# Filler multiplies of the identity on TensorE, at five changes of stage and in the two softmaxes of a sample attention

## The chip, the cores and the metric

The kernel runs on one core of a Trainium2 chip. The metric is the device time of one execution in microseconds. Three runs of the kernel before gave 2719.67, 2724.30 and 2724.41 us; the median is 2724.3 us. TensorE (PE in the profile) multiplies; its weight loads are a row of their own (PEld). VectorE (DVE), ScalarE (ACT) and GpSimd (POOL) do the element work, SyncE (SP) issues most DMAs. The profile also says which clock TensorE was granted: 1.00 stands for 2.4 GHz and 0.50 for 1.2 GHz.

## What is computed

One layer of a decoder for a prompt of 2048 tokens and 8 samples of 4 new tokens each, width 1024. Cut to what matters:

```python
h = rms_norm(x, norm1_g) * (1 + sc1) + sh1
q, k, v, u = split(h @ w_in)                 # w_in: 1024 x 2560
q, k = rms_norm(q per head), rms_norm(k per head)
o_attn = attend(q, k, v)                     # three dilated window patterns, merged by their softmax sums
glu = u[..., :512] * sigmoid(u[..., 512:])
o_conv = silu(layer_norm(causal_depthwise_conv31(glu))) @ w_pw2
x = x + g1 * (concat(o_attn, o_conv) @ w_o)
h2 = rms_norm(x, norm2_g) * (1 + sc2) + sh2
x = x + g2 * (square(relu(h2 @ w_ff1)) @ w_ff2)   # 1024 -> 4096 -> 1024
```

The prompt's attention works on its own keys, the samples' attention on a cache of 2048 positions each. The outputs are x, the new keys and values, and the last rows of glu.

## The kernel before

The work is cut into stages. Each is a block in which every engine has its own list of instructions in the order in which the code writes it; there is no scheduler. Semaphores join the lists. A tile is 128 tokens (`NT` = 16 tiles of the prompt, and a seventeenth of the 32 sample tokens). The stages are, with the prefix that their tiles carry in the profile:

1. `vu_`: modulation, first norm, the products for v and u, glu and most of the convolution;
2. `qk_`: the products for q and k, their norms, and their transposition. It starts with the sample tile: for each of 8 slices of the weights ACT writes the high part (`qk_w_hi`), DVE the low part (`qk_w_lo`, L1314), and TensorE multiplies as they come;
3. `pa_`: the prompt's attention. Beside it POOL gathers keys into `pa_key_run` (L1573) and does the rest of the convolution (L1577, L1578);
4. `sa_`: the samples' attention in two groups of four samples. For each group TensorE transposes cached keys (L1886), multiplies scores (L1898, L1905), then waits for a softmax on DVE and ACT, transposes the probabilities (`values`, L1911 to L1917) and multiplies them by the values (L1929, L1935);
5. `mx_`: mixing of the three patterns, convolution output, output projection, residual and second norm. The last step of TensorE is `turn_x(NT)` (L2435, transposes of L2441) for the sample tile;
6. `ff_`: the feed-forward products, from 1289 us to nearly the end.

Between two stages stands `end_stage()` (L125). The block's own end is a barrier: each engine first drains, that is, it finishes what it has been given, then reports, and goes on when all five have reported. Then the stage's semaphores are cleared, and a second barrier of the same kind follows (L129). An engine that is late at the first holds all the others. SP comes to the barrier only when the stores that the next stage reads have landed, or when they are issued, depending on the stage.

TensorE multiplies float32 numbers in two ways here. Where both operands carry the type fp32r, as in the large products, a call of `matmul` is one row of the trace; where they are plain float32, as in L1017, it is two rows. A `transpose` of float32 is one row.

In `qk_`, `turn_qk(NT)` (L1358) is the last step of TensorE: it waits for the tile's queries, transposes four blocks, waits for the keys (`nrm_done`), and transposes four more.

Of the kernel before, what the change touches and what calls it, by code (L numbers as in the profile page):

```python
# [15 lines left out]
P = 128  # L16
# [78 lines left out]
def build(nc, I, O):  # L95
# [22 lines left out]
    with whole:  # L118
# [15 lines left out]
        ident = keep("ident", [P, P])  # L134
# [32 lines left out]
        def copy_part(eng, i):  # L167

            n, part = divmod(i, COPY_PARTS)
            name, out = (("cache_k", "new_k_sample"), ("cache_v", "new_v_sample"))[n % 2]  # L170
            src = I[name][0, n // 2].rearrange("r h d -> (r h d)")[DS * AW:WINC * AW]
            dst = O[out][0, n // 2].rearrange("r h d -> (r h d)")[0:(WINC - DS) * AW]
            rows = slice(part * 16, (part + 1) * 16)
            a = 16 * COPY_PARTS
            eng.dma_start(dst.rearrange("(a n) -> a n", a=a)[rows], src.rearrange("(a n) -> a n", a=a)[rows]).then_inc(parts_copied, 16)

        class Chain:

# [41 lines left out]
        with conv:  # L220
# [454 lines left out]
            with ExitStack() as st:  # L675
# [35 lines left out]
                with nc.Block() as block:  # L711
# [252 lines left out]
                    def _(pe):  # L964
# [77 lines left out]
                        for i in range(2, NT + 1):  # L1042
# [6 lines left out]
                                partial(i)  # L1049
                            turn_glu(i - 1)  # L1050
                        turn_glu(NT)

            front.close()
            end_stage()
# [42 lines left out]
            with ExitStack() as st:  # L1097
# [47 lines left out]
                with nc.Block() as block:  # L1145
# [193 lines left out]
                    def _(pe):  # L1339
# [18 lines left out]
                        def turn_qk(u):  # L1358
                            n = rows_of(tile_at[u])
                            if u < NT:  # L1360
                                pe.wait_ge(nrm_done, u + 1)
                            if u >= 1:
                                pe.wait_ge(t_done, u)
                            for half in range(2):
                                if u == NT:
                                    if half == 0:
                                        pe.wait_ge(z_free, NT + 1)
                                    else:
                                        pe.wait_ge(nrm_done, NT + 1)
                                for c in range(4):  # L1370
                                    mm = pe.transpose(t_ps[:, half, c, 0:n], nrm[0:n, u % 2, (4 * half + c) * P:(4 * half + c + 1) * P], ident[0:n, 0:n])
                                mm.then_inc(t_pe, 1)

                        for u in range(NT):
                            products(u)
                            if u >= 2:
                                turn_qk(u - 2)
# [2 lines left out]
                        products(NT, (1,))  # L1380
                        turn_qk(NT - 1)
                        turn_qk(NT)

            end_stage()
            both.close()

            with ExitStack() as st:
# [111 lines left out]
                with nc.Block() as block:  # L1499
# [102 lines left out]
                    def _(pe):  # L1602
# [48 lines left out]
                        for s in range(STEPS + 4):  # L1651
                            if s < STEPS:
                                scores(2 * s)
                                scores(2 * s + 1)
                            if 1 <= s < STEPS + 1:
                                turn(2 * s - 2)
                                turn(2 * s - 1)
                            if s >= 4:
                                back(s - 4)
                            if 2 <= s < STEPS + 2:  # L1660
                                weigh(2 * s - 4)
                                weigh(2 * s - 3)

                    @block.vector
                    def _(v):
# [95 lines left out]
        with ExitStack() as st:  # L1761
# [26 lines left out]
            o_ps = ps("o_ps", [P, 512])  # L1788
# [20 lines left out]
            with nc.Block() as block:  # L1809
# [68 lines left out]
                def _(pe):  # L1878
# [27 lines left out]
                        mm.then_inc(s_pe, 1)  # L1906

                    def values(g):
                        pe.wait_ge(s_exp, 3 * g + 3)
                        for m in range(4):  # L1910
                            mm = pe.transpose(p_ps[1][:, m * P:(m + 1) * P], prob[:, 2, DS + m * P:DS + (m + 1) * P], ident[:])  # L1911
# [3 lines left out]
                            mm = pe.transpose(p_ps[0][:, m * P:(m + 1) * P], prob[:, 0, m * P:(m + 1) * P], ident[:])  # L1915
                        mm.then_inc(p_pe, 1)
                        pe.transpose(k_ps[0][0:DS, 0, :], prob[:, 0, 4 * P:SKEYS], ident[:]).then_inc(p_pe, 1)  # L1917
                        if g >= 1:
                            pe.wait_ge(o_done, g)
                        for a in range(2):  # L1920
                            if a == 0:
                                pe.wait_ge(p_cp, 2 * g + 2)
# [12 lines left out]
                                    pe.matmul(o_ps[part, :], probN[:, part], vnew[:, G * g + j, :], start=False, stop=False)  # L1935
                        mm.then_inc(o_pe, 1)

                    for g in range(DB // G):
                        for n in range(2 * G * g, 2 * G * (g + 1)):
                            for c in range(4):  # L1940
                                turn(n, c)
                            if n == 2 * G * g + G:
                                scores(2 * g)
                        scores(2 * g + 1)
                        values(g)

                @block.vector
                def _(v):
# [86 lines left out]
        with ExitStack() as st:  # L2035
# [57 lines left out]
            with nc.Block() as block:  # L2093
# [294 lines left out]
                def _(pe):  # L2388
# [77 lines left out]
                    for i in range(NT + 1):  # L2466
                        if i < NT:
                            turn_dw(i + 1)
                        project(i, 0)
                        if i < NT:  # L2470
                            turn_y(i + 1)
                            turn_o(i + 1)
                        project(i, 1)
                        if i >= 1:
                            turn_x(i - 1)
                    turn_x(NT)

        end_stage()
        lent.close()

        with ExitStack() as st:
# [199 lines left out]
            with nc.Block() as block:  # L2681
# [447 lines left out]
                def _(pe):  # L3129
# [19 lines left out]
                    def three(out, s, m, hi, lo, first, last, more=False):  # L3149
# [2 lines left out]
                        pe.matmul(out, w_hi[:, s % WR, w], lo, start=False, stop=False, skip_group_check=more)  # L3152
                        return pe.matmul(out, w_lo[:, s % WR, w], hi, start=False, stop=last, skip_group_check=more)  # L3153

                    for b in range(NB_ALL):
                        run, blk = divmod(b, BLKS)
                        w = RUNS[run][1]
# [112 lines left out]
```

## Time and profile before

| | |
|---|---|
| median of 3 runs | 2724.3 us |
| time of the profiled execution | 2723.36 us |
| its span, first to last instruction | 2721.5 us |
| PE busy | 2579.1 us (95%) |
| PEld busy | 2283.1 us (84%) |
| DVE, ACT, POOL busy | 1717.0, 1220.9, 1122.9 us |
| mean granted TensorE clock | 0.974 |

The span lies 1.9 us below the execution's own time. PE's busy share counts a matmul from its start to the end of its last result, so that neighbours overlap; it says that TensorE nearly always had something to do, not that it ran at its peak. The clock of 0.974 is a mean: it was 1.00 in most of the span and 0.50 in a handful of stretches of 3 to 27 us, the longest of them before 60 us, in the first stage.

### The profile page before, as it was taken

How to read it: one execution, taken by the hardware profiler on the slowest of the kernel's cores; microseconds unless marked ns; L12 is line 12 of the kernel's file. 1: busy time of each engine (PE TensorE's matmuls, PEld its weight loads, DVE VectorE, ACT ScalarE, POOL GpSimd, SP SyncE). 2: the span in 40 equal slices, each digit the busy share in tenths (PEclk: the TensorE clock that was granted, in tenths of full speed). 3: DMA queues.
4: the chain of work that ended last, by engine and by line, in shares of the span. 5: the costliest groups of instructions: out<-in, count | busy, mean ns of one | idle time of the engine just before them, and what ended most of it. 6: DMA issues, size and time to landing. Idle time of an engine off the chain costs nothing.

```text
span 2721.5 us, 45843 instructions
## 1 busy us (share of the span) xinstructions
PE 2579.1 (95%) x16346; PEld 2283.1 (84%) x16346; DVE 1717.0 (63%) x3931; ACT 1220.9 (45%) x3063; POOL 1122.9 (41%) x771
## 2 busy tenths in 40 slices
PE   6999989998999689997899999999999999999998
PEld 3678857876777546875899999999999999999998
DVE  3268889987888437875555555555555555555555
ACT  3444323458888324554434433433443343344332
POOL 0000000008997006653555545535554553555543
PEclk7999999998999889998999999999999999999999
DMA  8756625843445873673423443352454335235222
GB/s 287 276 201 230 206 104 199 269 128 113 137 137 160 301 313 121 196 240 93 146 75 136 171 137 117 100 195 71 139 171 136 117 105 186 82 131 190 78 63 82
DMA packets 314671, 431.24 MB, mean 158 GB/s; under 512 B 23546, under 2 KB 243430, under 8 KB 307910
## 3 DMA queue, kind: packets, MB, share of 16 engines
q1 hardware_dynamic: 292570, 378.88, 41.9%
q0 software_dynamic: 4272, 39.19, 4.1%
q10 hardware_dynamic: 17604, 10.24, 1.2%
q8 instruction: 133, 2.18, 0.3%
q14 instruction: 92, 0.75, 0.1%
HBM read 353.72 MB, written 146.65 MB: 184 GB/s over the span
## 4 chain that ended last, share of the span: by engine, by line
PE 43%; issue 2%; DVE 2%; DMA 2%; POOL 1%; ACT 1%; SPq 1%; DVEq 0%; POOLq 0%; ACTq 0%
PE ff_u_ps L3151 15%; PE ff_u_ps L3152 14%; PE ff_u_ps L3153 14%; DMA gluT<-h_d 1%; POOL ff_w_lo L2796 1%; DMA out_y_prompt_dram<-ff_x_own 0%; DVE ff_wT L3008 0%; SPq L2714 0%; ACT ff_h_hi L2853 0%; ACT ff_w_hi L2844 0%; POOL ff_h_lo L2805 0%; DMA ff_x_own<-x_d 0%; PE ff_out_ps L3146 0%; DVE ff_x_own L3033 0%; DVE ff_wT L2970 0%
## 5 line engine op out<-in xcount | busy, mean ns | idle before, releaser
L2796 POOL TENSOR_TENSOR ff_w_lo<-gluT,ff_w_hi 128x512 fp32r<-128x512 f32 x342 | 458.1, 1347 | 409.2 <-ACT ff_w_hi L2844 409.2
L3151 PE MATMUL ff_u_ps<-ff_a_hi,ff_w_hi 128*128 128x352 f32 (+1 forms) x1536 | 493.4, 321 | 10.7 <-POOL ff_a_lo L2811 8.8
L3152 PE MATMUL ff_u_ps<-ff_a_lo,ff_w_hi 128*128 128x352 f32 (+1 forms) x1536 | 493.5, 321 | 0.0
L3153 PE MATMUL ff_u_ps<-ff_a_hi,ff_w_lo 128*128 128x352 f32 (+1 forms) x1536 | 493.1, 321 | 0.0
L3151 PE MATMUL ff_u_ps<-ff_h_hi,ff_w_hi 128*128 128x352 f32 (+1 forms) x1368 | 441.4, 323 | 16.0 <-DVE ff_h_lo L2956 8.1
L3153 PE MATMUL ff_u_ps<-ff_h_hi,ff_w_lo 128*128 128x352 f32 (+1 forms) x1368 | 437.8, 320 | 0.0
L3152 PE MATMUL ff_u_ps<-ff_h_lo,ff_w_hi 128*128 128x352 f32 (+1 forms) x1368 | 437.1, 320 | 0.0
L3051 DVE SCALAR_TENSOR_TENSOR ff_y<-ff_u_ps,modT,ff_y 128x352 f32<-128x352 f32 (+2 forms) x336 | 188.2, 570 | 314.2 <-PE ff_u_ps L3153 314.2
L2796 POOL TENSOR_TENSOR ff_w_lo<-ff_wT,ff_w_hi 128x512 fp32r<-128x512 f32 x168 | 225.4, 1344 | 272.2 <-ACT ff_w_hi L2844 172.5
L2844 ACT ACTIVATE ff_w_hi<-gluT 128x512 fp32r<-128x512 f32 x342 | 211.4, 626 | 274.8 <-PE ff_u_ps L3153 257.4
L3151 PEld LDWEIGHTS ff_u_ps<-ff_a_hi,ff_w_hi 128*128 128x128 f32 x1536 | 290.5, 189 | 12.7 <-POOL ff_a_lo L2811 10.0
L3153 PEld LDWEIGHTS ff_u_ps<-ff_a_hi,ff_w_lo 128*128 128x128 f32 x1536 | 290.2, 189 | 0.0
L3152 PEld LDWEIGHTS ff_u_ps<-ff_a_lo,ff_w_hi 128*128 128x128 f32 x1536 | 290.1, 189 | 0.0
L3151 PEld LDWEIGHTS ff_u_ps<-ff_h_hi,ff_w_hi 128*128 128x128 f32 x1368 | 258.0, 189 | 23.4 <-issue 12.0
L3152 PEld LDWEIGHTS ff_u_ps<-ff_h_lo,ff_w_hi 128*128 128x128 f32 x1368 | 257.9, 189 | 0.0
L3153 PEld LDWEIGHTS ff_u_ps<-ff_h_hi,ff_w_lo 128*128 128x128 f32 x1368 | 256.9, 188 | 0.0
L2844 ACT ACTIVATE ff_w_hi<-ff_wT 128x512 fp32r<-128x512 f32 x168 | 105.6, 632 | 320.0 <-PE ff_u_ps L3153 234.6
L1735 ACT ACTIVATE pa_score<-pa_score,pa_stat 128x256 f32<-128x256 f32 (+1 forms) x384 | 172.3, 451 | 36.3 <-DVE pa_stat L1680 34.6
L287 DVE SCALAR_TENSOR_TENSOR vu_dwp<-gluT,tapT,vu_dwp 128x512 f32<-128x512 f32 x240 | 161.0, 745 | 0.8 <-DVE rstd L204 0.8
L985 PE MATMUL vu_z_ps<-vu_w_hi,last_hi 128*128 128x512 f32 (+1 forms) x384 | 152.0, 396 | 2.5 <-DVEq L923 2.5
L986 PE MATMUL vu_z_ps<-vu_w_lo,last_hi 128*128 128x512 f32 (+1 forms) x384 | 150.3, 391 | 0.0
L987 PE MATMUL vu_z_ps<-vu_w_hi,last_lo 128*128 128x512 f32 (+1 forms) x384 | 150.0, 391 | 0.0
(354 smaller groups left out, 5016.3 us busy)
## 6 DMA issues: line engine op xcount, KB each, us to landing
gluT<-in_w_ff_dram SPq DMA_DIRECT2D x192, 512.0 KB, 5.0
out_new_k_sample_dram<-in_cache_k_dram SPq DMA_DIRECT2D x40, 511.0 KB, 6.1
out_new_v_sample_dram<-in_cache_v_dram SPq DMA_DIRECT2D x40, 511.0 KB, 6.3
dwq<-in_w_ada_dram SPq DMA_DIRECT2D x32, 512.0 KB, 8.8
gluT<-in_cache_k_dram SPq DMA_DIRECT2D x16, 1024.0 KB, 8.6
gluT<-h_d SPq DMA_DIRECT2D x80, 176.0 KB, 5.2
mx_acc<-acc_d SPq DMA_DIRECT2D x16, 768.0 KB, 8.1
out_new_k_sample_dram<-in_cache_k_dram POOLq DMA_DIRECT2D x3, 4088.0 KB, 16.6
```

Of the source, the lines that this page charges most:

```text
L287: return v.scalar_tensor_tensor(out=out, in0=x, scalar=tap(j, c), in1=out, op0=ALU.mult, op1=ALU.add)
L985: pe.matmul(z, hi, w_hi[:, k, cols], start=k == 0, stop=False)
L986: pe.matmul(z, hi, w_lo[:, k, cols], start=False, stop=False)
L987: mm = pe.matmul(z, lo, w_hi[:, k, cols], start=False, stop=k == KT - 1)
L1735: act.activation(prob[:, u % 4, hh, cols], score[:, u % 4, hh, cols], ACT.Exp, bias=stat[:, p, t, 0, h:h + 1], scale=-1.0, accum_out=stat[ ...
L2796: pool.tensor_tensor(slot_view(w_lo, s), src, slot_view(w_hi, s).bitcast(F32), ALU.subtract).then_inc(w_lod, 1)
L2844: act.activation(slot_view(w_hi, s), src, ACT.Copy).then_inc(w_hid, 1)
L3051: ins = v.scalar_tensor_tensor(out=dst, in0=src[:, 0:gated], scalar=g2, in1=dst, op0=ALU.mult, op1=ALU.add)
L3151: pe.matmul(out, w_hi[:, s % WR, w], hi, start=first, stop=False, skip_group_check=more)
L3152: pe.matmul(out, w_hi[:, s % WR, w], lo, start=False, stop=False, skip_group_check=more)
L3153: return pe.matmul(out, w_lo[:, s % WR, w], hi, start=False, stop=last, skip_group_check=more)
```

## The change

A helper issues `n` plain float32 multiplies of the 128 x 128 identity by itself, into a part of PSUM that nobody reads any more or yet. It is called at twelve places: behind the last step of TensorE in the first five stages (24, 30, 30, 34 and 24 calls of `matmul`), at the start of three stages (8, 8 and 12), ahead of the last half of `turn_qk(NT)` (18), ahead of `turn_x(NT)` in `mx_` (50), and twice in each of the two softmaxes (26 and 8). In `values` the wait for `o_done` moves to the front, since the fillers write the bank that this semaphore guards. Nothing is removed.

```diff
+        def keep_awake(pe, out, n):
+
+            for _ in range(n):
+                pe.matmul(out, ident[:], ident[:], start=True, stop=True)
@@ end of vu_ @@
                         turn_glu(NT)
+                        keep_awake(pe, xt_ps[:, 0], 24)
@@ qk_, turn_qk @@
                                     if half == 0:
                                         pe.wait_ge(z_free, NT + 1)
                                     else:
+                                        keep_awake(pe, z_ps[0][:, 0:P], 18)
                                         pe.wait_ge(nrm_done, NT + 1)
@@ qk_, start and end @@
+                        keep_awake(pe, z_ps[5][:, 0:P], 8)
                         for u in range(NT):
                             products(u)
...
                         turn_qk(NT)
+                        keep_awake(pe, z_ps[0][:, 0:P], 30)
@@ end of pa_ @@
+                        keep_awake(pe, s_bank[0][0][:, 0:P], 30)
@@ sa_, values @@
                     def values(g):
+                        if g >= 1:
+                            pe.wait_ge(o_done, g)
+                        keep_awake(pe, o_ps[:, 0:P], 26)
                         pe.wait_ge(s_exp, 3 * g + 3)
...
                         pe.transpose(k_ps[0][0:DS, 0, :], prob[:, 0, 4 * P:SKEYS], ident[:]).then_inc(p_pe, 1)
-                        if g >= 1:
-                            pe.wait_ge(o_done, g)
+                        keep_awake(pe, o_ps[:, 0:P], 8)
@@ sa_, start and end @@
+                    keep_awake(pe, o_ps[:, 0:P], 8)
                     for g in range(DB // G):
...
                         values(g)
+                    keep_awake(pe, k_ps[1][:, 0], 34)
@@ end of mx_ @@
+                    keep_awake(pe, dw_ps[:, 0:P], 50)
                     turn_x(NT)
+                    keep_awake(pe, dw_ps[:, 0:P], 24)
@@ start of ff_ @@
+                    keep_awake(pe, out_ps[:, 0:P], 12)
```

The order in which the instructions stand on TensorE at three of the places follows. A row is a line of the code, an operation, output and inputs, and how many times in a row; the numbers at the left count rows. After the change all later lines have higher numbers (L1371 is L1378, L1911 is L1924, L2441 is L2455); the fillers are L180.

TensorE at the end of `qk_` and the start of `pa_`, before: `qk_t_ps` holds the transposed queries and keys.

```order
2144 L1355 MATMUL qk_z_ps<-qk_w_hi,last_lo 128x512
2145 L1371 MATMUL qk_t_ps<-ident,qk_nrm 128x128 x16
2146 L1145 UNCONDITIONAL_BRANCH
2147 L1601 UNCONDITIONAL_BRANCH
2148 L1615 MATMUL pa_s_ps<-first_k,first_q 128x128 x2
```

The same place after the change:

```order
2146 L1361 MATMUL qk_z_ps<-qk_w_hi,last_lo 128x512
2147 L1378 MATMUL qk_t_ps<-ident,qk_nrm 128x128 x12
2148 L180 MATMUL qk_z_ps<-ident 128x128 x18
2149 L1378 MATMUL qk_t_ps<-ident,qk_nrm 128x128 x4
2150 L180 MATMUL qk_z_ps<-ident 128x128 x30
2151 L1151 UNCONDITIONAL_BRANCH
2152 L1610 UNCONDITIONAL_BRANCH
2153 L1624 MATMUL pa_s_ps<-first_k,first_q 128x128 x2
```

Of the last sixteen transposes the last four now stand behind 18 fillers, and the way to the barrier behind 30.

TensorE in the first softmax of `sa_`, before: `sa_s_ps` are the scores, `sa_k_ps` the transposed probabilities, `sa_o_ps` the output.

```order
2556 L1898 MATMUL sa_s_ps<-sa_kTt,sa_qblk 32x512 x16
2557 L1911 MATMUL sa_k_ps<-ident,sa_prob 128x128 x4
2558 L1915 MATMUL sa_k_ps<-ident,sa_prob 128x128 x4
2559 L1917 MATMUL sa_k_ps<-ident,sa_prob 4x128
2560 L1929 MATMUL sa_o_ps<-first_v,sa_probT 32x512 x3
```

The same place after the change:

```order
2563 L1908 MATMUL sa_s_ps<-sa_kTt,sa_qblk 32x512 x16
2564 L180 MATMUL sa_o_ps<-ident 128x128 x26
2565 L1924 MATMUL sa_k_ps<-ident,sa_prob 128x128 x4
2566 L1928 MATMUL sa_k_ps<-ident,sa_prob 128x128 x4
2567 L1930 MATMUL sa_k_ps<-ident,sa_prob 4x128
2568 L180 MATMUL sa_o_ps<-ident 128x128 x8
2569 L1941 MATMUL sa_o_ps<-first_v,sa_probT 32x512 x3
```

The transposes of the probabilities stand behind 26 fillers, the products with the values behind 8 more.

TensorE at the end of `mx_` and the start of `ff_`, before: `mx_h_ps` holds the transposed second norm.

```order
3495 L2441 MATMUL mx_h_ps<-ident,mx_x1n 128x128 x8
3496 L2441 MATMUL mx_h_ps<-ident,mx_x1n 128x32 x8
3497 L2093 UNCONDITIONAL_BRANCH
3498 L3128 UNCONDITIONAL_BRANCH
3499 L3151 MATMUL ff_u_ps<-ff_h_hi,ff_w_hi 128x352
```

The same place after the change:

```order
3507 L2455 MATMUL mx_h_ps<-ident,mx_x1n 128x128 x8
3508 L180 MATMUL mx_dw_ps<-ident 128x128 x50
3509 L2455 MATMUL mx_h_ps<-ident,mx_x1n 128x32 x8
3510 L180 MATMUL mx_dw_ps<-ident 128x128 x24
3511 L2107 UNCONDITIONAL_BRANCH
3512 L3144 UNCONDITIONAL_BRANCH
3513 L180 MATMUL ff_out_ps<-ident 128x128 x12
3514 L3167 MATMUL ff_u_ps<-ff_h_hi,ff_w_hi 128x352
```

The sample tile's eight transposes stand behind 50 fillers, the barrier behind 24, and the first product of `ff_` behind 12.

## Rows read from the trace of the kernel before

**Rows 1.** Windows: length, busy PE, PEld, DVE, ACT, POOL, granted clock, DMA share, GB/s.
```profile
394.00:412.00 18.00, 9.78 (x24) 3.17 (x25) 11.08 (x18) 8.13 (x8) 0.00 (x0) 0.62 0.59 206
...
sum 85.00, PE 43.44 PEld 27.66 DVE 33.39 ACT 28.78 POOL 13.79; mean PE 6.21 PEld 3.95 DVE 4.77 ACT 4.11 POOL 1.97
```

**Rows 2.** Group of line L1017 (busy us, mean ns), and weight loads by start.
```profile
L1017 PE MATMUL vu_q_ps<-vu_sel,vu_part 128*128 128x9 f32 x48 | 6.3, 241 | 0.0
...
162.96 0.53 PEld L1017 LDWEIGHTS vu_q_ps<-vu_sel,vu_part 128*128 128x128 f32 x4
163.40 0.19 PEld L985 LDWEIGHTS vu_z_ps<-vu_w_hi,last_hi 128*128 128x128 f32 x1
```

**Rows 3.** From `vu_` to `qk_`: instructions by start, duration; a wait of SP.
```profile
392.84 1.01 SPq L771 DMA_DIRECT2D out_new_conv_sample_dram<-vu_glu  x1
393.56 0.40 PE L996 MATMUL vu_g_ps<-ident,vu_glu 32*128 32x32 f32 x4 [1.64 <-DVE gluT L940]
397.36 1.06 ACT L1259 ACTIVATE qk_w_hi<-dwq 128x1024 fp32r<-128x1024 f32 x1 [5.25 <-PEq L129]
...
SPq L776 <- DMA out_new_conv_sample_dram<-vu_glu: 2.2, 1, 2.2
```

**Rows 4.** From `qk_` to `pa_`, in order of time.
```profile
611.25 0.66 PE L1371 MATMUL qk_t_ps<-ident,qk_nrm 128*128 128x128 f32 x4 [3.03 <-ACT qk_qkT L1233]
615.26 1.12 PE L1371 MATMUL qk_t_ps<-ident,qk_nrm 128*128 128x128 f32 x4 [3.35 <-DVE qk_nrm L1310]
620.99 2.01 POOL L1573 COPY pa_key_run<-first_k 128x1024 f32<-128x1024 f32 x1 [119.70 <-POOLq L129]
```

**Rows 5.** In `pa_`, a wait of PE and POOL's first gap.
```profile
750.09 1.23 PE L1615 MATMUL pa_s_ps<-pa_key_run,pa_query_run 64*128 64x128 f32 x8 [2.81 <-POOL pa_key_run L1573]
...
865.93 1.98 POOL L1573 COPY pa_key_run<-pa_kT 128x1024 f32<-128x1024 f32 x1 [1.60 <-PE pa_s_ps L1615]
```

**Rows 6.** From `pa_` to `sa_`, PE.
```profile
901.90 0.41 PE L1648 MATMUL pa_o_ps<-ident,pa_oT 128*128 128x128 f32 x2 [0.61 <-DVE pa_o_sb L1697]
908.05 1.30 PE L1886 MATMUL sa_k_ps<-ident,gluT 128*128 128x128 f32 x5 [5.74 <-PEq L129]
```

**Rows 7.** The first softmax of `sa_`, in order of time.
```profile
941.08 3.64 PE L1898 MATMUL sa_s_ps<-sa_kTt,sa_qblk 128*32 128x512 f32 x32
948.17 1.11 PE L1911 MATMUL sa_k_ps<-ident,sa_prob 128*128 128x128 f32 x4 [3.45 <-ACT sa_prob L2016]
950.86 0.27 DVE L1985 COPY sa_probN<-sa_k_ps 4x128 f32<-4x128 f32 x1
951.18 1.08 PE L1929 MATMUL sa_o_ps<-first_v,sa_probT 128*32 128x512 f32 x3 [0.83 <-DVE sa_probN L1985]
952.04 1.07 PE L1929 MATMUL sa_o_ps<-first_v,sa_probT 128*32 128x512 f32 x3
954.93 0.60 PE L1929 MATMUL sa_o_ps<-first_v,sa_probT 128*32 128x512 f32 x3
955.36 0.60 PE L1929 MATMUL sa_o_ps<-first_v,sa_probT 128*32 128x512 f32 x3
```

**Rows 8.** From `sa_` to `mx_`, in order of time.
```profile
1001.45 0.61 PE L1929 MATMUL sa_o_ps<-sa_vn,sa_probT 128*32 128x512 f32 x3
1003.95 2.70 SPq L1852 DMA_DIRECT2D os_d<-sa_o_r  x4
1009.94 0.60 ACT L2247 ACTIVATE gluT<-mx_f_ps 128x512 f32<-128x512 f32 x1 [18.80 <-PE mx_f_ps L2450]
```

**Rows 9.** From `mx_` to `ff_`, in order of time.
```profile
1271.63 1.03 PE L2441 MATMUL mx_h_ps<-ident,mx_x1n 128*128 128x128 f32 x8
1281.09 1.05 PE L2441 MATMUL mx_h_ps<-ident,mx_x1n 32*128 32x32 f32 x8 [8.43 <-DVE mx_x1n L2325]
1284.92 0.58 SPq L2148 DMA_DIRECT2D h_d<-gluT  x1
1286.84 0.63 ACT L2844 ACTIVATE ff_w_hi<-gluT 128x512 fp32r<-128x512 f32 x1 [9.42 <-PEq L129]
```

## The prediction, made before the changed kernel ran

> **What bounds the kernel now.** I read the page first, then the granted clock in windows over the whole span, then, at each place that the change touches, the timeline of every engine across the gap. The first view shows that TensorE has nearly always something to do; the second, what there is to win. From 394 us on, seven stretches with a lowered clock lie at the places of the change. Together they last 85 us, and PE is busy in 43.4 of them [rows 1]; the first has a mean clock of 0.62, the others are like it. Work at the lower level takes twice as long, so a clock that never fell could give back half of the busy time, some 20 us, and that only where PE's work sets the pace. The timelines then show what does set the pace in each gap: a store that SP waits for, a norm on DVE, a softmax on ACT, or the barrier. In front of these PE is idle for 3 to 8 us. A filler is free as long as it ends before what PE waits for; each 0.1 us beyond is paid in full, since a barrier holds five engines. So the question is how long a filler lasts.
>
> **The price of a filler.** Of L1017, a plain float32 multiply with 128 x 128 weights, the trace has 48 rows [rows 2]; the code calls it 24 times (two calls for each of twelve groups). A call is two rows, two weight loads and two matmuls. Four such loads, two calls, take from 162.96 to 163.40 us, so 0.11 us a row at full clock. With 128 columns to move, as the filler has, eight float32 rows of L2441 take 1.03 us, (1.03 - 0.27) / 7 = 0.11 us each with 0.27 us for the last one's end [rows 9]. Loads and matmuls overlap, so a row costs 0.11 and a call 0.22 us. No row shows both sizes in one plain multiply. The lower bound is one row a call, 0.11 us; the upper is a load that hides behind nothing, 0.11 + 0.11 a row, 0.44 a call. I take 0.22, which both nearest rows give.
>
> The Trainium skill ("TensorE: Matmul & The Clock Gate", Part 2, on the back-to-back issue gap) gives about 56 ns for a single matmul of 128 columns at full clock and 81 ns for a pair of load and matmul in a stream. By the first, estimated, 24 calls would last 1.3 us and no filler would end late; the time would be that of the first rival below. The trace does not agree for this kind: two calls of L1017 took 0.44 us [rows 2], and the measurement decides.
>
> **The barrier.** Before 397.36 SP had issued its last store at 392.84 + 1.01 and waited 2.2 us for it: it arrived at 396.05 and ACT began 1.31 us later [rows 3]. At 1284.92 + 0.58 = 1285.50 SP had issued the last store of `mx_`, and ACT began 1.34 us later [rows 9]. So the next stage begins 1.33 us after the last engine arrives. PE arrives when its last matmul has ended, 0.16 us after its last slot (0.27 less 0.11).
>
> **Place by place**, fillers at 0.22 us:
>
> 1. `vu_` to `qk_`: PE is free at 393.8. 24 calls, 5.3 us, end at 399.3 against the arrival of SP at 396.05: **+3.2**. What then starts later is ACT's and DVE's splitting of weights, from which PE's first products wait; a warm PE only waits longer there. The 8 calls at the start, 1.8 us, stand beside ACT's 1.06 us and DVE's first split: at most 0.5 more, taken as 0.
> 2. `turn_qk(NT)` and the end of `qk_`: the first four transposes end at 611.25 + 0.44. 18 calls, 4.0 us, end at 615.7 where the keys had been waited for until 615.26: 0.4 late, and the four cold transposes (1.12 us, the last 0.42 of it an end) become 0.3 us faster or more. That cancels. From 616.1 the 30 calls last 6.6 us, to 622.9; the others arrive at 620.99 - 1.33 = 619.7 [rows 4]: **+3.2**.
> 3. In `pa_` the first 6 us run faster at full clock, 2 to 3 us of PE's work. But POOL works without a gap from 620.99 to its first wait, ahead of 865.93, and at 750.09 PE waits 2.8 us for POOL's `pa_key_run` [rows 5]. What PE gains before is waiting time there: **0**. This hides the gain, and if POOL were not the pace, up to 3 us would come back.
> 4. `pa_` to `sa_`: PE is free at 902.1; 30 calls end at 908.9 against 908.05 - 1.33 = 906.7 [rows 6]: **+2.2**. The 8 calls ahead of the first transposes stand beside loads that DVE waits for: 0.
> 5. The first softmax: the scores end at 944.5 (eight slots of 0.43 us from 941.08). 26 calls last to 950.2, where the probabilities were ready at 948.17 [rows 7]: 2.0 late. Nine warm transposes end at 951.2, 8 calls at 953.0, and DVE's copy is ready before; the products with the values begin 1.8 us later than at 951.18. Their first four slots are then warm: 952.04 - 951.18 = 0.86 becomes 955.36 - 954.93 = 0.43, 1.7 us won. Net **+0.1**. The second softmax, 982 to 1002 us, repeats the pattern with 3.5 cold slots: **+0.3**.
> 6. `sa_` to `mx_`: PE is free at 1001.9; 34 calls, 7.5 us, and the end of the last: 1009.5 against SP's arrival at 1003.95 + 2.70 = 1006.65 [rows 8]: **+2.9**. In `mx_` the first transposes are warm, and ACT, which paces the next 3 us, starts its first copy some 0.85 us earlier than 1009.94: **-0.85**.
> 7. Ahead of `turn_x(NT)`: PE is free at 1271.63 + 0.88 = 1272.5. 50 calls, 11.0 us, end at 1283.5; the norm was ready at 1281.09 [rows 9]: 2.4 late, less 0.5 as these transposes are now warm. The path on is DVE, SP's store, barrier. But behind the transposes, at 1284.0, stand 24 calls, 5.3 us, to 1289.5 with their end. The arrival was 1285.50: **+4.0**. The 12 calls at the start of `ff_` last 2.7 us, as long as PE has to wait for ACT and DVE there: 0.
>
> The sum: 3.2 + 3.2 + 2.2 + 0.1 + 0.3 + 2.9 - 0.85 + 4.0 = 15.05 us. On the profiled execution's own 2723.36 us that is 2738.4, and since the median of the runs is 0.9 us above it I forecast **2739 us**. `ff_` runs as before. Where its pace falls on the clock's own steps, a few us of PE at 1333 or 2289 us may turn warm or cold by chance: +-2 us.
>
> **Rivals.**
>
> A. The fillers fit. A call costs one row's 0.11 us, because the plain multiply of so small a size is one slot. Then the 24 calls end at 396.7 (+0.6), the 18, 26, 30, 34, 50 and 24 all before what is waited for. Each softmax wins 2.6 us (0.9 in the transposes, 1.7 in the products), `mx_` 0.85, the end of `qk_` 0.4 and `turn_x(NT)` 0.5: 0.6 - 5.2 - 1.75 = -6.35, **2718 us**. For it: all the gaps in question are 1.2 to 2 times as long as the fillers at that price. Against it: the 48 rows for 24 calls [rows 2]. The point from which it decides is a price of 0.17 us a call: there the places 1, 2, 4, 6 and 7 run over by 2.0, 1.3, 0.7, 1.2 and 0.4 us and the softmaxes by 0.75 each, 7.1 in all, against 7.0 won. Below it the kernel is not slower.
>
> B. The clock falls all the same, before or within a filler, and the filler runs at the lower level, 0.44 us a call. The likeliest place is ahead of the 18 calls, where PE has been idle for 3.0 us [rows 4]. If the 30 calls there and the 24 of place 1 run cold, 6.6 + 5.3 us more: **2750 us**.
>
> C. The late stage catches up. `sa_` waits for its loads and `ff_` for its own, and what had been issued ahead of the barrier goes on while PE fills. If both take their whole delay back, 2.2 + 4.0 less: **2733 us**. Against it: SP stands at the barrier as well and issues nothing.
>
> **Chances.** Forecast 0.66 (its own range 2732 to 2745), A 0.14, B 0.08, C 0.12. The range that leaves out no more than 2 in 10 is 2724 to 2752: it cuts off A, and holds B and C with the clock's steps. What a measurement of this kernel can tell from no change is 0.2%, 5.4 us, so from 2718.9 to 2729.7. A lies at its lower edge and goes two thirds to faster, one third to the same; the low end of C and half-fitting fillers add to the same: faster 0.10, same 0.09, slower 0.81.
>
> **What would show it.** In the profile after, L180 has 612 rows for 306 calls, starts 0.11 us apart. The clock is 1.00 at 613 to 627, 947 to 955, 988 to 996 and 1275 to 1293 (all shifted). The next stage begins 1.3 us after the last L180 at the five changes of stage. `pa_` from POOL's first row to PE's last is as long as before, with a longer wait at the place of 750. I am wrong if L180 has 306 rows, if its rows start less than 0.07 us apart, or if stages begin while the fillers run. A lowered clock within the fillers would be B.

## The result and the profile after

The changed kernel takes **2741.1 us** (median of 4 runs, 2740.75 to 2741.21) against 2724.4 us before (4 runs, 2719.67 to 2726.86): a ratio of **1.0070**, 95% interval 1.0056 to 1.0083. Forecast were 2739 us with a range of 2724 to 2752, and 0.81 for slower. The profiled execution of the changed kernel took 2740.75 us, with a span of 2738.7 us and a mean granted clock of 0.985, where the one before had 2721.5 us and 0.974. So the clock was kept better and the kernel is slower all the same: its span is 17.2 us longer.

The fillers have line L180 now. The other lines have moved by 5 to 16 numbers.

The first rows are the place from `vu_` to `qk_` [rows 3]: start, duration, engine, line, tile and count of the rows, in brackets the idle time before and what ended it. The window row behind them has the granted clock third from its end.

```profile
393.27 1.02 SPq L776 DMA_DIRECT2D out_new_conv_sample_dram<-vu_glu  x1
393.99 0.40 PE L1001 MATMUL vu_g_ps<-ident,vu_glu 32*128 32x32 f32 x4 [1.64 <-DVE gluT L945]
394.32 7.25 PE L180 MATMUL vu_xt_ps<-ident 128*128 128x128 f32 x48
402.48 2.96 ACT L1265 ACTIVATE qk_w_hi<-dwq 128x1024 fp32r<-128x1024 f32 x3 [9.95 <-PEq L129]
...
395.50:398.50 3.00, 3.00 (x16) 3.00 (x16) 0.00 (x0) 0.00 (x0) 0.00 (x0) 0.50 0.11 40
```

24 calls are 48 rows, as forecast. They last 7.25 us and not 5.3, since the clock is at its lower level (0.50, 1.2 GHz) in the middle of them, and the next stage begins 0.91 us after their end at 401.57. Right ahead of them PE had waited 1.64 us.

From `qk_` to `pa_` [rows 4]:

```profile
616.26 0.66 PE L1378 MATMUL qk_t_ps<-ident,qk_nrm 128*128 128x128 f32 x4 [3.94 <-ACT qk_qkT L1239]
616.75 5.81 PE L180 MATMUL qk_z_ps<-ident 128*128 128x128 f32 x36
622.40 0.60 PE L1378 MATMUL qk_t_ps<-ident,qk_nrm 128*128 128x128 f32 x4
622.84 6.86 PE L180 MATMUL qk_z_ps<-ident 128*128 128x128 f32 x60
630.53 4.06 POOL L1582 COPY pa_key_run<-first_k 128x1024 f32<-128x1024 f32 x2 [125.33 <-POOLq L129]
```

The 18 calls ran at the lower level for 3.4 us and lasted 5.8 us in place of 4.0; the second four transposes no longer wait for a norm but stand behind fillers.

In `pa_`, the wait at the place of 750, a window with a lowered clock and POOL's first long gap [rows 5]:

```profile
759.64 0.71 PE L1624 MATMUL pa_s_ps<-pa_key_run,pa_query_run 64*128 64x128 f32 x8 [2.81 <-POOL pa_key_run L1582]
...
832.00:836.00 4.00, 3.78 (x26) 3.05 (x28) 2.04 (x11) 1.82 (x9) 3.92 (x3) 0.57 0.61 164
...
876.94 1.98 POOL L1582 COPY pa_key_run<-pa_kT 128x1024 f32<-128x1024 f32 x1 [3.00 <-PE pa_s_ps L1624]
```

Up to 759.6 POOL sets the pace, as forecast: 2.81 us of waiting, to the hundredth as before. But behind a lowered stretch at 832 us, where none was before, POOL's gap grows from 1.60 to 3.00 us: here POOL waits for PE.

From `pa_` to `sa_` [rows 6], in PE's timeline and in the list of SP's waits (us in total, times, longest):

```profile
912.90 0.41 PE L1657 MATMUL pa_o_ps<-ident,pa_oT 128*128 128x128 f32 x2 [0.61 <-DVE pa_o_sb L1707]
913.15 6.86 PE L180 MATMUL pa_s_ps<-ident 128*128 128x128 f32 x60
921.69 0.95 POOL L1877 MEMSET sa_qblk<- 128x1024 f32 x1 [30.74 <-POOLq L129]
...
SPq L1567 <- DMA st_d<-pa_stat: 4.6, 1, 4.6
```

Here the fillers end at 920.01, and `sa_` begins 1.68 us later: in this one place a store of SP was the last to arrive. Its wait of 4.6 us was 2.8 us before.

The first softmax [rows 7], and the start of `mx_` [rows 8], on PE and ACT:

```profile
955.22 3.64 PE L1908 MATMUL sa_s_ps<-sa_kTt,sa_qblk 128*32 128x512 f32 x32
958.79 6.07 PE L180 MATMUL sa_o_ps<-ident 128*128 128x128 f32 x52
964.70 0.60 PE L1924 MATMUL sa_k_ps<-ident,sa_prob 128*128 128x128 f32 x4
965.68 1.95 PE L180 MATMUL sa_o_ps<-ident 128*128 128x128 f32 x16
...
1027.29 0.60 ACT L2261 ACTIVATE gluT<-mx_f_ps 128x512 f32<-128x512 f32 x1 [19.54 <-PE mx_f_ps L2464]
```

From `mx_` to `ff_` [rows 9]:

```profile
1286.92 1.03 PE L2455 MATMUL mx_h_ps<-ident,mx_x1n 128*128 128x128 f32 x8
1287.79 11.33 PE L180 MATMUL mx_dw_ps<-ident 128*128 128x128 f32 x100
1299.05 0.68 PE L2455 MATMUL mx_h_ps<-ident,mx_x1n 32*128 32x32 f32 x8
1299.66 5.62 PE L180 MATMUL mx_dw_ps<-ident 128*128 128x128 f32 x48
1306.24 0.63 ACT L2860 ACTIVATE ff_w_hi<-gluT 128x512 fp32r<-128x512 f32 x1 [13.53 <-PEq L129]
```

100 rows in 11.33 us, less 0.27 us for the last one's end, are 0.112 us a row: **0.223 us a call**. The same stretches of both timelines, laid side by side, say where the 17.2 us lie. Each is the difference of two intervals between the same two instructions.

| stretch | before | after | difference | forecast |
|---|---|---|---|---|
| start to the last glu transposes of `vu_` | 393.56 | 393.99 | +0.4 | 0 |
| place 1, to ACT's first row of `qk_` | 3.80 | 8.49 | +4.7 | +3.2 |
| place 2, to POOL's first row of `pa_` | 223.63 | 228.05 | +4.4 | +3.2 |
| place 3, to PE's last rows of `pa_` | 280.91 | 282.37 | +1.5 | 0 |
| place 4, to POOL's first row of `sa_` | 6.11 | 8.79 | +2.7 | +2.2 |
| to the first scores | 33.07 | 33.53 | +0.5 | 0 |
| place 5, both softmaxes, to the last products | 60.37 | 61.76 | +1.4 | +0.4 |
| place 6, to SP's first load of `mx_` | 6.47 | 9.16 | +2.7 | +2.9 |
| `mx_` to `turn_x(NT-1)` | 263.71 | 260.78 | -2.9 | -0.85 |
| place 7, to ACT's first row of `ff_` | 15.21 | 19.32 | +4.1 | +4.0 |
| `ff_` | 1434.66 | 1432.46 | -2.2 | 0 |

### The profile page after: what moved, and what is told of

Its sections match the earlier page's. It is cut to its first block, busy times and chain, and to the rows that moved or that the text cites. A ratio compares the mean times of both kernels' runs of the same rounds, so it can differ in the third digit from the quotient of the medians.

```text
span 2738.7 us, 47067 instructions
## 1 busy us (share of the span) xinstructions
PE 2637.6 (96%) x16958; PEld 2344.7 (86%) x16958; DVE 1717.5 (63%) x3931; ACT 1220.4 (45%) x3063; POOL 1123.3 (41%) x771
## 4 chain that ended last, share of the span: by engine, by line
PE 43%; issue 2%; DVE 2%; DMA 2%; POOL 1%; SPq 1%; ACT 1%; DVEq 0%; POOLq 0%; ACTq 0%
PE ff_u_ps L3167 14%; PE ff_u_ps L3169 14%; PE ff_u_ps L3168 14%; DMA gluT<-h_d 1%; POOL ff_w_lo L2812 1%; SPq L2730 1%; DMA out_y_prompt_dram<-ff_x_own 0%; DVE ff_wT L3024 0%; DMA ff_x_own<-x_d 0%; ACT ff_h_hi L2869 0%; PE ff_out_ps L3162 0%; DVE ff_x_own L3049 0%; ACT ff_w_hi L2860 0%; POOL ff_h_lo L2821 0%; DVE ff_wT L2987 0%
## 5 line engine op out<-in xcount | busy, mean ns | idle before, releaser
L1745 ACT ACTIVATE pa_score<-pa_score,pa_stat 128x256 f32<-128x256 f32 (+1 forms) x384 | 172.4, 451 | 37.7 <-DVE pa_stat L1690 35.8
```

What stands on the lines that cost most here:

```text
L1745: act.activation(prob[:, u % 4, hh, cols], score[:, u % 4, hh, cols], ACT.Exp, bias=stat[:, p, t, 0, h:h + 1], scale=-1.0, accum_out=stat[ ...
```

## Experiments

My theory was the prediction's own: fillers are too long by their second row, and what runs over a wait is paid in full. Its rival was that filling costs or gives something of its own: a clock that falls all the same, a gain that never comes, a fixed price at a barrier. All ratios are to the kernel before on the same chip in the same rounds. Single runs of the kernel before range over 0.5% on one chip (2719.8 to 2733.7 us in 32 runs), so a ratio near 1 is told to about 0.1%.

To compare what the clock costs, I read the granted clock and PE's busy time in half-microsecond windows over the whole span, and summed the busy time with the kernel's own work (fillers taken off) at the lowered clock behind 100 us. Before, that is 57.8 us; after, 23.7 us.

### Half the calls

```diff
-keep_awake(pe, xt_ps[:, 0], 24)
+keep_awake(pe, xt_ps[:, 0], 12)
```
and so at all twelve places.

> Every filler count halved (12, 9, 4, 15, 15, 13, 4, 4, 17, 25, 12, 6). Theory 'overrun': the change loses because a call lasts 0.226 us and the fillers end behind what is waited for; the kept clock itself is worth something. Halved, all fillers end in time but those behind vu_ (12 calls, 2.7 us, some 0.4 us late). Left are the gains: 2.6 us in each softmax, 0.9 to 2.9 in mx_, up to 2 in ff_: 2714 to 2719 us, faster than before (2724) by 0.2 to 0.4%. Rival 'idle clock': a half-filled gap lets the clock fall and nothing is won, 2722 to 2726 us. Rival 'cost is not length' (the rows on PE disturb others whatever their number): half of the loss stays, about 2732 us.

Measured: 1.0001 (0.9991 to 1.0011), 2727.0 us over 12 runs. The loss of the change is gone, but so is the gain I had expected.

```profile
388.93 4.57 PE L180 MATMUL vu_xt_ps<-ident 128*128 128x128 f32 x24
608.53 3.68 PE L180 MATMUL qk_z_ps<-ident 128*128 128x128 f32 x18
612.59 3.51 PE L180 MATMUL qk_z_ps<-ident 128*128 128x128 f32 x30
```

12 calls should have lasted 2.7 us; they lasted 4.6, as the clock fell within them too. Own work at the lowered clock: 39.4 us in 14 stretches, where before there had been 57.8 in 12.

### Transposes in place of multiplies

```diff
-pe.matmul(out, ident[:], ident[:], start=True, stop=True)
+pe.transpose(out, ident[:], ident[:])
```

> Full counts, but each filler is a transpose of the identity and not a multiply: one row of 0.11 us where the multiply has two. Theory 'overrun': the same lengths as with halved counts, so the same time within 2 us, 2714 to 2719 us, if transposes hold the granted clock as multiplies do. Rival: transposes do not hold it; then the clock falls in the gaps as before and the time is 2722 to 2726 us. If a call's cost were not its rows' length but its issue, 2741 us as the changed kernel.

Measured: 1.0000 (0.9987 to 1.0013).

```profile
387.22 2.84 PE L180 MATMUL vu_xt_ps<-ident 128*128 128x128 f32 x24
```

24 calls are 24 rows now, and (2.84 - 0.27) / 23 = 0.112 us each: a row costs the same, and the plain float32 multiply issues two. That settles the price. At the lowered clock are 35.8 us of own work, so (57.8 - 35.8) / 2 = 11 us could have come back. The time is that of the rival, transposes that don't hold the clock, but its mechanism isn't there: over the ten runs the mean granted clock is 0.985, against 0.974 before. In the profile `sa_` is 4.0 us shorter and `mx_` 0.8 us longer, but `ff_` is 1442.4 us against 1434.7, with lowered stretches at 1322, 1824 and 2285 us. In this profile the gain was won ahead of `ff_` and lost in it. The clock is only a part of that: PE also waits 5.7 us for DVE's `ff_y` there, where it waited 1.8 us before.

### Only the ends, only the inside

One kernel keeps the fillers at the ends and starts of stages (24, 8, 30, 30, 8, 34, 24, 12), the other the 18, 26, 8 and 50 within stages:

```diff
-keep_awake(pe, dw_ps[:, 0:P], 50)
 turn_x(NT)
 keep_awake(pe, dw_ps[:, 0:P], 24)
```

> Only the fillers behind the last step of the five stages and at three starts, at full counts; none in turn_qk, the softmaxes and ahead of turn_x. Theory 'overrun': five late barriers, 4.7 + 2.8 + 2.3 + 2.8 + 1.9 us, less some 5 us won in mx_ and ff_: 2734 us. Rival 'the loss is inside the stages': 2724 to 2728 us.

> Only the fillers inside stages at full counts (18, 26 and 8 twice, 50). Theory 'overrun': 0.4 to 2 us late in turn_qk, 0.4 in the two softmaxes together, 2.4 ahead of turn_x: 2727 to 2729 us. Rival 'the loss is inside the stages': 2735 to 2741 us. Rival 'what the softmaxes win outweighs': under 2722 us.

Measured: 1.0038 (1.0026 to 1.0051) and 1.0016 (1.0003 to 1.0029). That is some 10 and 4 us, as the theory had it. The sum, 1.0054, is near the whole, 1.0070. The ends are the larger part. With no filler ahead of it the last one even ran cold, 8.53 us for the 24 calls that took 5.62 us behind the 50:

```profile
1287.08 8.53 PE L180 MATMUL mx_dw_ps<-ident 128*128 128x128 f32 x48
```

### The ends doubled

```diff
-keep_awake(pe, k_ps[1][:, 0], 34)
+keep_awake(pe, k_ps[1][:, 0], 68)
```
and 48, 60, 60 and 48 at the other four ends.

> The changed kernel with the counts at the five ends of stages doubled (48, 60, 60, 68 and 48 calls in place of 24, 30, 30, 34 and 24), everything else as changed. My theory: PE is already the last to arrive at each barrier, so each added call is paid in full at 0.226 us (2 rows of 0.113 us): 142 calls x 0.226 = 32.1 us over the changed kernel, 2773 us against its 2741, a ratio to the kernel before of 1.019 (up to 3 us more if a lowered clock falls inside a longer filler, 1.7 us per such 3.4 us stretch). Rival, the time is a fixed price of a stage whose end PE keeps open (something that starts late, whatever the length): no more than 2745 us, ratio 1.007. Rival, the late stage catches up: loads go on while PE fills, so only part is paid, 2760 us or less.

Measured: 1.0154 (1.0134 to 1.0173), 2769.0 us over 4 runs (2763.8 to 2775.4); the profiled one is the slowest.

```profile
394.21 12.61 PE L180 MATMUL vu_xt_ps<-ident 128*128 128x128 f32 x96
629.49 13.56 PE L180 MATMUL qk_z_ps<-ident 128*128 128x128 f32 x120
1037.12 15.45 PE L180 MATMUL sa_k_ps<-ident 128*128 128x128 f32 x136
```

The five barriers moved by 5.36, 6.70, 5.89, 7.60 and 5.36 us against the changed kernel, 30.9 in all for 142 calls. Four of the five are 0.223 us a call. The third (`pa_` to `sa_`) gives 0.8 us less, which is what SP's store had held there already. So in this profile each call is paid in full, and no fixed price stands beside it. The ratio over all runs, 1.0154 less 1.0070, is 23 us with 7 to either side: less than the 32 expected, and I can't say from one profile where the other executions were shorter.

### The moved wait alone

```diff
     def values(g):
+        if g >= 1:
+            pe.wait_ge(o_done, g)
         pe.wait_ge(s_exp, 3 * g + 3)
...
-        if g >= 1:
-            pe.wait_ge(o_done, g)
```

> No filler at all; what is left of the change is that the wait for o_done stands ahead of the transposes of the second group's softmax instead of behind them. All theories: no difference to the kernel before, ratio 1.000 +- 0.001, stages as long as before (qk_ to pa_ 223.6, pa_ to sa_ 287.0, sa_ to mx_ 99.9 us). If it is slower by 1 us or more in sa_, the moved wait has a price of its own and the fillers less. Its other use: it shows how far two kernels with equal work differ.

Measured: 1.0000 (0.9989 to 1.0011). It costs nothing. Its profile also shows how far equal work differs by itself: the start of `qk_` lies at 392.3 us in place of 397.4, and `sa_` lasts 101.7 in place of 99.9 us.

### Transposes in the softmaxes only; a filled wait in `ff_`; both

The first kernel has only the 26 and 8 calls of each softmax, as transposes. The second has only a new filler in `ff_`, where PE waits longest for POOL:

```diff
+if b == 0:
+    keep_awake(pe, out_ps[:, 0:P], 32)
 pe.wait_ge(alo_d, 8 * b + 6)
```

The third has both.

> Fillers only in the two softmaxes of the sample attention, and as transposes of the identity (one row of 0.118 us a call): 26 calls last 3.1 us where PE waits 3.5 us or more, 8 last 0.9 us. Theory (a filler that ends in time gives what the kept clock gives): from the scores to the last product with the values 60.37 us before becomes 57.1 us, as it was with all fillers as transposes; ratio 0.9985 to 0.999 (-3.3 us on 2727). Rival (the clock falls anyway, a little later, onto work): the same stretch 60 us, ratio 1.000.

> Only the 32 transposes in ff_ ahead of the wait of 4.4 us for POOL's low half; no other filler. Theory (the gain of the run before, 0.9963, is that of ff_, the softmaxes gave nothing by themselves): ff_ lasts 1432 to 1433 us, as there, against 1434.7 in the profile of before and up to 1442 where a lowered stretch comes at some 1827 us; ratio 0.997 (0.996 to 0.998). Rival (the two together keep the clock by where they put it, neither alone): ff_ 1435 to 1441 us, ratio 0.999 to 1.000.

> As the run with transposes in the softmaxes only, and beside that 32 transposes (3.8 us) in ff_ ahead of the wait for the fifth and sixth low half of the first block, where PE waits 4.4 us for POOL and the clock is lowered right behind it for 6.8 us with 6.2 us of PE's work in it. Theory (a filled wait keeps the clock): that stretch goes, 3.1 us less in ff_, and with the softmaxes 0.9975 to 0.998 (-5.5 to -6.5 us). Rival (ff_ follows DVE and POOL there, and what PE wins becomes a longer wait for ff_y; or the lowered stretch comes at another place with full work in it): no more than the softmaxes give, 0.9985 to 1.000.

Measured: softmaxes alone **1.0001** (0.9990 to 1.0012, 12 runs), `ff_` alone **1.0010** (0.9996 to 1.0023, 12 runs), both **0.9963** (0.9950 to 0.9976, 6 runs). Neither theory had that. Since six runs are few, the third kernel ran again on another chip:

> The same kernel as the run with 26 and 8 transposes in the softmaxes and 32 in ff_ (ratio 0.9963, 0.9950 to 0.9976, from six runs), once more, since neither half of it alone gave anything (1.0001 and 1.001). If the two together keep the clock in a way that neither does alone, the ratio is again 0.995 to 0.9975 and ff_ lasts 1432 us with no lowered stretch in it. If the six runs were luck, the ratio is 0.998 to 1.001 and ff_ lasts 1435 us or more.

Measured: **0.9958** (0.9945 to 0.9970), 2714.8 us against 2726.9 before. It is real. The window rows (length, busy PE, PEld, DVE, ACT, POOL, clock, DMA share, GB/s) show `ff_` with the softmaxes alone, and then with both, in the profile of the second time:

```profile
1325.00:1333.00 8.00, 4.36 (x17) 4.36 (x18) 7.50 (x9) 3.89 (x9) 4.77 (x4) 0.57 0.00 1
1827.00:1831.00 4.00, 4.00 (x16) 4.00 (x17) 4.00 (x10) 0.00 (x0) 0.00 (x0) 0.57 0.00 0
2288.00:2292.00 4.00, 4.00 (x18) 4.00 (x18) 2.75 (x8) 0.48 (x1) 0.00 (x0) 0.60 0.00 0
```

```profile
1318.67 3.66 PE L180 MATMUL ff_out_ps<-ident 128*128 128x128 f32 x32
...
1325.08 0.43 PE L3167 MATMUL ff_u_ps<-ff_a_hi,ff_w_hi 128*128 128x352 f32 x1 [1.80 <-POOL ff_a_lo L2827]
...
1318.00:1330.00 12.00, 10.20 (x75) 9.90 (x74) 11.05 (x15) 6.30 (x14) 6.71 (x6) 1.00 0.23 69
1797.00:1820.00 23.00, 20.97 (x130) 20.38 (x129) 13.47 (x24) 6.06 (x13) 6.58 (x6) 1.00 0.33 109
2270.00:2294.00 24.00, 21.35 (x138) 20.81 (x137) 14.39 (x29) 6.95 (x16) 7.51 (x6) 1.00 0.31 102
```

The table has, for these kernels and the two of the next experiment, the interval from the scores to the last products with the values (`sa_`), `ff_` with the number of lowered stretches in it behind 1300 us (in brackets), the kernel's own work at the lowered clock behind 100 us, and the ratio.

| kernel | `sa_` | `ff_` | own work, low | ratio |
|---|---|---|---|---|
| moved wait alone | 62.1 | 1434.7 (2) | 59.6 | 1.0000 |
| softmaxes | 59.6 | 1440.8 (3) | 55.1 | 1.0001 |
| `ff_` | 62.1 | 1439.7 (3) | 59.8 | 1.0010 |
| both | 55.6 | 1432.0 (0) | 46.4 | 0.9963 |
| both, again | 56.7 | 1428.3 (0) | 36.9 | 0.9958 |
| both, and the end of `sa_` | 58.7 | 1436.4 (3) | 56.8 | 0.9967 |
| all places, fitted, and `ff_` | 59.6 | 1433.6 (1) | 34.1 | 0.9974 |

The ratios are of 5 to 12 runs each, the other columns of one profile each; that of "both, again" is the fastest of its six runs (2708.1 us). The granted clock of all runs goes with the ratios: against the kernel before on the same chip its mean is higher by 0.001 with the softmaxes, by 0.000 with the filler of `ff_`, and by 0.0035 and 0.005 with both. So the two together hold the clock better than either. The mean clock alone does not make the time, though: with transposes at all twelve places it was higher by 0.0105, and the ratio was 1.0000.

Where the gain lies the profiles don't settle. The filler in `ff_` runs over 300 us behind the softmaxes, so it did not shorten `sa_` in the same execution. The 4.0 us between 59.6 and 55.6 are 1.5 us of a longer wait for a load and a lowered stretch with 3.2 us of work in it. The kernel with the end of `sa_` filled beside both has the longer wait too (3.04 us), and takes 58.7 us. The row behind that wait, with the softmaxes alone and then with both, the first time:

```profile
967.14 3.47 PE L1896 MATMUL sa_k_ps<-ident,gluT 128*128 128x128 f32 x16 [3.20 <-DMA gluT<-in_cache_k_dram]
...
965.71 1.97 PE L1896 MATMUL sa_k_ps<-ident,gluT 128*128 128x128 f32 x16 [1.73 <-DMA gluT<-in_cache_k_dram]
```

Nor is the clock the whole of the 8.8 us by which `ff_` with the softmaxes alone is longer than with both. Half of the 10.3 us of work in its three stretches is 5.2 us. Beside that PE waits longer for DVE's `ff_y`. The row of that wait behind 1813 us and the line of all such waits (us in total, times, longest), with the softmaxes alone and then with both, the first time:

```profile
1826.86 0.55 PE L3167 MATMUL ff_u_ps<-ff_a_hi,ff_w_hi 128*128 128x352 f32 x1 [2.05 <-DVE ff_y L3065]
...
PE ff_u_ps L3167 <- DVE ff_y L3065: 6.0, 3, 2.4
```

```profile
1821.51 0.43 PE L3167 MATMUL ff_u_ps<-ff_a_hi,ff_w_hi 128*128 128x352 f32 x1 [0.29 <-DVE ff_y L3065]
...
PE ff_u_ps L3167 <- DVE ff_y L3065: 1.6, 3, 0.9
```

The stretch at 1827 us comes right behind this wait of 2.05 us, and the one at 1824 us of the kernel with twelve transposes behind one of 1.80 us for the same tile. In the kernel before no wait for this tile is longer than 0.9 us, and it has no stretch there. With half the calls the wait was 1.58 us, and no stretch came. The stretches near 2288 us come right behind a wait for POOL of 1.9 us, which the kernels without that stretch have as well. Behind 1400 us all 13 lowered stretches of the fourteen profiles (but for the last instructions) begin 0.1 to 1.5 us behind a wait of 1.8 to 2.1 us. So a stretch there follows a wait of some 2 us, but such a wait does not always bring one.

Why the two fillers together do what neither does, no run of mine shows. I did not try the filler of `ff_` beside others than these, nor an equal number of instructions that fill nothing. That stays open.

### Fillers that fit at all places, and one more end

One kernel has transposes at all twelve places, with counts meant to end before what is waited for (20, 24, 8, 26, 36, 28, 8, 8, 44, 70, 24, 12), and the filler in `ff_`. The other is the best kernel with the end of `sa_` filled beside it:

```diff
+keep_awake(pe, k_ps[1][:, 0], 44)
```

> All twelve places with transposes (0.118 us a call), the counts such that each ends just before what is waited for (20, 24, 8, 26, 36, 28, 8, 8, 44, 70, 24 and 12), and the 32 transposes in ff_. Theory (what the change loses is length alone; in length that fits, the kept clock is a gain where PE sets the pace): no change of stage longer than before by over 0.5 us, sa_ 4 us and ff_ 3 us shorter, at most 30 us of the kernel's own work at the lowered clock after 100 us (57.8 before, 35.8 with unfitted transposes); ratio 0.9945 to 0.996. Rival (the clock falls after each filler for 3.4 us onto work that would have stood in a wait otherwise): the gain is that of ff_ alone, 0.997.

> That same kernel with 44 transposes (5.2 us) more at the end of sa_, where PE waits 5.5 us and more before mx_. Theory (a filler that fits keeps the clock for the first work of mx_): from the start of mx_ to turn_x(NT-1) 260.8 us, as with the 34 multiplies, against 263.7 before, and no later start of mx_: 2 to 3 us less than its sibling, ratio 0.9955. Rival (the lowered stretch only moves): mx_ as long as in the sibling, ratio 0.9963 or above.

Measured: 0.9974 (0.9963 to 0.9986) and 0.9967 (0.9954 to 0.9980). Both are faster than the kernel before, and neither beats the kernel with fillers at only three places. The first of the two is at its rival's figure (0.997), not at its theory's (0.9945 to 0.996), and its fillers do not all fit: at place 1 the 20 transposes took 4.00 us, partly at the lower level, and the next stage began 1.4 us later than before.

In this kernel the wait of 8.4 us ahead of `turn_x(NT)` is filled with 70 transposes, and the clock is whole throughout:

```profile
1265.51 7.80 PE L180 MATMUL mx_dw_ps<-ident 128*128 128x128 f32 x70
...
1264.60:1279.40 14.80, 12.16 (x111) 11.61 (x109) 6.08 (x30) 4.06 (x10) 2.91 (x2) 1.00 0.21 52
```

Before, that wait and what follows had 17.1 us of lowered clock. The Trainium skill ("TensorE: Matmul & The Clock Gate", Part 4) holds that the full clock doesn't engage for transposes. By that rule the clock would have fallen here; the trace doesn't agree.

`mx_` is 3.0 us shorter in this profile and 2.2 us shorter in the other, as with the multiplies. But this kernel still has 34.1 us of its own work at the lowered clock: among it 5.7 us right at the start of `ff_`. There it cost nothing, as far as the rows show: both this kernel and the one before come to their next wait for POOL's `ff_h_lo` 11.4 to 11.5 us behind ACT's first row, and the one before had waited 0.87 us for DVE on the way.

## Why the prediction was right, and where its terms were off

**The price of a filler: right.** Two rows a call, 0.112 us each, 0.223 against the 0.22 forecast. The kernel with one row a call lost nothing, and in the profile with double counts the barriers moved by that price.

**The barrier: the principle right, the size off.** Each 0.1 us beyond the wait is paid in full. But where PE is the last, the next stage begins 0.77 to 0.95 us after the last filler's end (0.91 at place 1), not 1.33; the 1.33 us had been read where SP's store was last. At place 4 SP was last although PE ended at 920.0, since its store took 4.6 us in place of 2.8.

**Places 1 and 2: mis-sized**, +4.7 and +4.4 against +3.2 each. Rival B held in part: the clock was low for 3.4 us within the 24 and the 18 calls, so that they lasted 1.9 and 1.8 us longer, and the barriers took back 0.4 and 0.5 us of it. So the clock was not 1.00 at 613 to 627 us (shifted), as the prediction had it. With half the calls it was low within the fillers of both places too. PE had waited 1.6 and 3.9 us right ahead of them, and a filler behind a wait does not always undo it: the 24 transposes at place 1, behind the same 1.64 us, ran at the full clock. With doubled calls the stretch at place 1 was no longer than with single ones. I had given that 0.08 as a rival, and nothing as a term.

**Place 3: the hiding was right, the zero was not.** At the place of 750 all is as forecast. The +1.5 us is that of a lowered stretch 202 us into `pa_`. Of fourteen profiles five have one 201 to 204 us in (after, half the calls, doubled ends, both, and its sibling with one end more), and PE's last rows come 282.4 to 282.6 us behind POOL's first. The other nine have their stretches 188 to 196 us in, or earlier, or none, and take 280.8 to 281.0 us. So `pa_` hides a cold stretch at one place and not at another.

**Place 5: a little off**, +1.4 against +0.4. The products with the values begin 2.2 us late in each softmax, not 1.8, and the warm slots behind them give back 1.6 and 1.4 us of it, some 0.2 us less than worked out.

**Places 6 and 7: right**, +2.7 against +2.9 and +4.1 against +4.0.

**`mx_`: mis-sized**, -2.9 against -0.85. I had let ACT pace its first microseconds, by the one interval at 1009.94. But all of PE's 4.4 us at the lowered clock at 1006 to 1012 us seem to have counted, half of which is 2.2 us; the other 0.7 us no run explains. The five profiles with no lowered stretch behind the start of `mx_` are 1.5 to 2.9 us shorter up to `turn_x(NT-1)`.

**`ff_`: 0 against -2.2**, hardly more than the 2 us given to chance. The spread I gave was too small: `ff_` lasts from 1428 to 1442 us over fourteen profiles in which its own work is the same.

The terms that were too low sum to 6.6 us, those too high to 4.5. That the total came out only 2 us off is in part luck, by their cancelling: with no gain in `mx_` beyond the forecast and none in `ff_` it would have been over 6 us off, still within the range. Of the rivals, A fell (612 rows), C fell (with doubled ends nothing was given back at the barriers), and B was there in part.

The part of the prediction that the experiments do not bear out is an aside: that a clock which never fell "could give back half of the busy time". After the change the kernel's own work at the lowered clock is 34 us less, worth up to 17 us, and with one-row fillers 22 us less, worth 11. Of the 11 nothing was left in the median. By the profiles part fell in `pa_`, where POOL sets the pace, and part was lost in `ff_`, to stretches and to longer waits for DVE's `ff_y`. Before, the lowered stretches lay over waits: PE was busy in 58 of 99 us. With fillers they are fewer and lie over work: with transposes 36 of own work and 6 of fillers in 48 us.

## To carry to other kernels

A filler must end before what PE waits for; count the rows that a call issues (two for a plain float32 multiply, one for a transpose, 0.112 us each here), fill only the part of the wait that is surely there, and reckon with a cold filler behind an earlier wait. Fill those waits behind which PE sets the pace, and expect little of the rest: three such places gave 0.4% here, and adding the others, fitted, gave nothing more (0.3%). The twelve places without the one in `ff_` gave nothing or cost 0.7%. And time the parts together as well as singly, in several runs each: here fillers at two spots that gave nothing alone gave 10 to 11 us together, and a single profile could not have told either.

## What the runs showed of the hardware

- The clock fell within running fillers: 395.5 to 398.5 us at 0.50 with PE busy all of it. Being busy now did not keep the clock where PE had waited 1.64 us just before; 24 transposes behind the same wait, in another kernel, kept it.
- The lowered stretches in `ff_` behind 1400 us began 0.1 to 1.5 us behind waits of 1.8 to 2.1 us; five profiles have a wait of 1.9 us near 2288 us (shifted) and no stretch behind it.
- 70 transposes of the identity kept the clock at 1.00 over a wait of 8.4 us, as the 50 multiplies did.
- A plain float32 multiply of 128 x 128 by 128 columns took two rows and 0.223 us, a float32 transpose of that size one row and 0.112 us.
- Up to the last transposes of `vu_`, ahead of every edit, the profiles took from 386.9 to 394.0 us, and `ff_` took from 1428 to 1442 us. Such a spread hides a gain of 5 us in any single profile.
- The time from PE's last matmul at a barrier to the next stage's first row was 0.77 to 0.95 us, where that from SP's last store was 1.3 us and more.
